# The order of VectorE's modulation sums and routing shift in the first block of a three-block model

## The reference

```python
mod = silu(c) @ w_ada + b_ada                    # 6 x 1024 values
shift1, scale1, gate1, shift2, scale2, gate2 = split(mod, 6)
h = rms_norm(x, norm1_g) * (1 + scale1) + shift1
q, k, v, u, z_gate = split(h @ w_in)
y_attn = attention(q, k, v) @ w_branch_attn
y_pool = pool_mixer(u) @ w_branch_pool
g_attn, g_pool = split(sigmoid(z_gate + b_gate), 2)
mixed = (g_attn * y_attn + g_pool * y_pool) @ w_out
x = x + gate1 * mixed
h2 = rms_norm(x, norm2_g) * (1 + scale2) + shift2
y_moe = experts(h2)                              # router: h2 @ [w_group, w_expert]
x = x + gate2 * y_moe
```

## Time and profile before

| what | value |
|---|---|
| median of 3 timed runs | 1359.34 us (1358.04 to 1361.08) |
| profiled execution | 1357.77 us |
| its span | 1356.0 us |
| busy: TensorE matmul | 1318.7 us (97%) |
| busy: VectorE | 657.4 us (48%) |
| busy: ScalarE | 292.7 us (22%) |
| read from HBM | 359.02 MB, 266 GB/s over the span |
| mean granted TensorE clock | 0.997 |

### The profile page before, as it was taken

One profiled execution on the slowest core, in us unless ns is written; L12 is line 12 of the kernel. 1 busy time (PEld: TensorE's weight loads), 2 busy tenths in 40 slices (PEclk: granted clock), 3 DMA queues, 4 the chain that ended last, 5 costly groups with the idle time before them and its releaser, 6 DMA issues.

```text
span 1356.0 us, 21295 instructions
## 1 busy us (share of the span) xinstructions
PE 1318.7 (97%) x8834; PEld 996.1 (73%) x8834; DVE 657.4 (48%) x1493; ACT 292.7 (22%) x601; POOL 7.8 (1%) x18
## 2 busy tenths in 40 slices
PE   8999899999999999888999999999999999999997
PEld 5999785453443443333688789999998878999997
DVE  6897565121001001000568647775545773867454
ACT  2223102112121121111343611210014361122000
POOL 0000000000000000000000000000000000000000
PEclk9999999999999999999999999999999999999999
DMA  9997797999999999999964054444544414544510
GB/s 389 407 363 260 314 421 308 424 413 422 421 422 421 422 421 422 422 421 421 388 215 141 32 186 156 169 174 159 183 156 141 150 54 155 173 170 161 182 63 32
DMA packets 52099, 364.63 MB, mean 269 GB/s; under 512 B 6161, under 2 KB 6465, under 8 KB 8994
## 3 DMA queue, kind: packets, MB, share of 16 engines
q1 hardware_dynamic: 49392, 355.49, 66.3%
q10 hardware_dynamic: 1890, 5.04, 1.2%
q0 software_dynamic: 720, 2.72, 0.5%
HBM read 359.02 MB, written 2.11 MB: 266 GB/s over the span
## 4 chain that ended last, share of the span: by engine, by line
PE 82%; DMA 13%; DVE 3%; issue 1%; SPq 1%; ACT 0%; DVEq 0%; ACTq 0%
PE bank L1220 31%; PE bank L921 19%; PE bank L667 14%; DMA ring<-in_weights 10%; PE bank L932 3%; PE bank L679 3%; DMA ringx<-in_weights 2%; PE bank L1365 2%; PE bank L1136 2%; PE bank L757 1%; PE bank L906 1%; PE bank L1269 1%; DVE ring L1845 1%; PE bank L1320 1%; PE bank L1346 1%
## 5 line engine op out<-in xcount | busy, mean ns | idle before, releaser
L921 PE MATMUL bank<-ring,cst 128*64 128x512 f32 x600 | 167.6, 595 | 7.1 <-DMA ring<-in_weights 5.7
L1220 PE MATMUL bank<-h,ring 128*128 128x128 f32 x1056 | 134.8, 276 | 1.2 <-DVE small L1818 0.6
L1220 PEld LDWEIGHTS bank<-h,ring 128*128 128x128 f32 x1056 | 126.1, 192 | 2.5 <-issue 2.4
L2165 DVE TENSOR_TENSOR act<-act,bank 128x512 f32<-128x512 f32 (+1 forms) x17 | 11.1, 656 | 239.9 <-PE bank L921 239.9
L667 PE MATMUL bank<-h,ring 128*128 128x256 f32 x576 | 127.1, 380 | 0.1
L667 PEld LDWEIGHTS bank<-h,ring 128*128 128x128 f32 x576 | 108.8, 190 | 15.3 <-issue 0.5
L921 PEld LDWEIGHTS bank<-ring,cst 128*64 128x64 f32 x600 | 52.5, 137 | 91.4 <-issue 89.6
L1220 PE MATMUL bank<-hid,ring 128*128 128x128 f32 x912 | 115.6, 275 | 0.0
L1220 PEld LDWEIGHTS bank<-hid,ring 128*128 128x128 f32 x912 | 108.6, 192 | 0.0
L1220 PE MATMUL bank<-sq,ring 128*128 128x128 f32 x720 | 95.1, 275 | 0.0
L921 PE MATMUL bank<-ringx,cst 128*64 128x512 f32 x256 | 90.3, 595 | 3.8 <-DMA ring<-in_weights 2.3
(11 more groups left out here) (425 smaller groups left out, 1935.7 us busy)
## 6 DMA issues: line engine op xcount, KB each, us to landing
ring<-in_weights SPq DMA_DIRECT2D x251, 1024.0 KB, 10.6
ringx<-in_weights SPq DMA_DIRECT2D x44, 1024.0 KB, 22.9
spare<-in_weights SPq DMA_DIRECT2D x18, 1024.0 KB, 21.2
pool_a<-in_weights SPq DMA_DIRECT2D x9, 1024.0 KB, 23.1
x<-in_weights SPq DMA_DIRECT2D x9, 1024.0 KB, 22.5
ring<-in_weights SPq DMA_DIRECT2D x6, 512.0 KB, 19.6
x<-in_x SPq DMA_DIRECT2D x1, 1024.0 KB, 4.9
pool_a<-in_cst ACTq DMA_DIRECT2D x1, 1024.0 KB, 20.4
```

Of the source, the lines that this page charges most:

```text
L921: ins = e.matmul(g.bank[bank][ex * SLOTS:(ex + 1) * SLOTS, :], stat(m, ex), pair[ex][:, m * 512:(m + 1) * 512], start=first and m == 0, st ...
L1220: ins = e.matmul(u.ap[:, at * P:(at + 1) * P], stat[:, k, :], moving[:, k, :], start=k == 0 and (of == 1 or (b == 0 and first)), stop=k == ...
```

## The change

The change reorders VectorE's instructions. It adds and removes no work, and leaves the other engines' programs and the list of loads alone.

- Gate loop: the modulation sums of tiles 12, 13, 14, 15 stand at j = 1, 3, 4, 5 instead of 1, 3, 5, 7, and at j = 4 behind the bounds.
- The routing shift stands at j = 6 instead of behind the loop, with the sum of tile 16 between its two instructions.
- Attention loop: the sums of tiles 17, 18, 19 ahead of chunks 0, 3, 6, instead of 16 and 17 ahead of chunks 0 and 4.
- Pool loop: the sums of tiles 20 and 21 ahead of chunks 2 and 6, instead of 18 and 19 ahead of chunks 0 and 4.
- Output loop: the sums of tiles 22 and 23 ahead of chunks 0 and 2, instead of 20 to 23 ahead of chunks 0 to 3.

```diff
         if j < 6:
             dve_first_sums(e, g, 6 + j)
-        if j % 2 == 1:
-            dve_ada(e, g, 12 + j // 2)
         if j == 4:
             dve_bounds(e, g)
-
-    modulated(e, g, 15)
-    e.tensor_tensor(g.shift_parts.rearrange("p (k r) -> p k r", k=KC), g.p("w_router").rearrange("p (k r) -> p k r", k=KC),
-                    g.mod[:, 24:32].unsqueeze(2).to_broadcast([P, KC, 36]), ALU.mult).then_inc(s["shift_routed"], 1)
-    e.wait_ge(s["shift_routed"], 1)
-    e.tensor_reduce(g.shift_sum, g.shift_parts.rearrange("p (k r) -> p r k", k=KC), AX.X, ALU.add).then_inc(s["shift_routed"], 1)
+        if j in (1, 3, 4, 5):
+            dve_ada(e, g, (12, 13, 14, 15)[(1, 3, 4, 5).index(j)])
+        if j == 6:
+            modulated(e, g, 15)
+            e.tensor_tensor(g.shift_parts.rearrange("p (k r) -> p k r", k=KC), g.p("w_router").rearrange("p (k r) -> p k r", k=KC),
+                            g.mod[:, 24:32].unsqueeze(2).to_broadcast([P, KC, 36]), ALU.mult).then_inc(s["shift_routed"], 1)
+            dve_ada(e, g, 16)
+            e.wait_ge(s["shift_routed"], 1)
+            e.tensor_reduce(g.shift_sum, g.shift_parts.rearrange("p (k r) -> p r k", k=KC), AX.X, ALU.add).then_inc(s["shift_routed"], 1)
+
     mixed = g.h
     e.wait_ge(s["gated"], 16)
     for oc in range(KC):
-        if oc % 4 == 0:
+        if oc % 3 == 0:
             if oc == 0:
...
-            dve_ada(e, g, 16 + oc // 4)
+            dve_ada(e, g, 17 + oc // 3)
...
     for oc in range(KC):
-        if oc % 4 == 0:
-            dve_ada(e, g, 18 + oc // 4)
+        if oc in (2, 6):
+            dve_ada(e, g, 20 + oc // 4)
...
     for oc in range(KC):
-        if oc < 4:
-            dve_ada(e, g, 20 + oc)
+        if oc in (0, 2):
+            dve_ada(e, g, 22 + oc // 2)
         if oc > 1:
```

## The result

| | kernel before | changed kernel |
|---|---|---|
| median | 1359.33 us (22 runs) | 1361.23 us (22 runs) |
| ratio of the runs | | 1.0014, 95% interval 1.0008 to 1.0020 |
| profiled execution | 1357.77 us | 1361.76 us |
| its span | 1356.0 us | 1360.0 us |
| first load of L584 | 226.05 | 230.07 |

The change makes the kernel slower by 1.9 us, 0.14%, with 1.1 to 2.7 us as the interval. One of the 22 runs of the kernel before took 1515.83 us; without it the median is 1359.32. The lowest runs, 1357.56 and 1359.65, are 2.1 us apart, the two profiled executions 4.0 us. These differences have to be explained, and what lies between them is the instructive part. The last two rows answer: whatever the change does, it does before the experts, and nothing is lost or won behind them.

A forecast was written before the change was run, and what follows sets the result against it. The prediction took the DMA stream to bound the experts, so only TensorE's begin of them counts: 4.6 - 1.5 = +3.1, plus 1.3 for the clock, is +4.4 on 1359.34, so 1363.7 us; range 1358.5 to 1367.6.

The forecast's parts named there:

- One for one through the experts: Experts: the DMA stream never stops, so the kernel's end moves one for one with TensorE's begin of the experts.
- Part 1: Gates and routing shift: TensorE doesn't stop at L798, attention branch and weight stream start earlier, minus 1.45 us.
- Part 2: Attention and pool loops: sums wait for their tiles, tile 21 lands at 179.15, mixture ends at 183.2, 6.6 us later.
- Parts 3 and 4: Output product: chunk 0 held by the last mixture chunks, plus 4.6 us; output loop: stall for scaled chunk 3 gone, minus 1.5.
- the 3 or more given as a sign: Output product: TensorE shows a new wait for L1924, the mixture's last chunks, of 3 us or more.
- The sum of +3.1: Begin of the experts: 4.6 - 1.5 = +3.1 us, 199.67 becoming 202.8, clock not included.
- Part 5: TensorE's clock falls after its idle time before 182.4, in the output run: costs 0 to 1.9 us, taken as 1.3.
- the shift is the same for both: Whole kernel: +4.4 us applies alike to the profiled execution (1357.77) and the timed median (1359.34), giving 1363.7.
- slower by over 0.2%: Whole kernel: slower by more than 0.2%, which is 2.7 us; chance 0.69.
- half of it: Rival: tile 21 lands sooner, without its 1.3 us delay, and the clock doesn't fall: +1.8 us, 1361.1; chance 0.12.
- not slower: Rival: banks hide VectorE's holds, mixture done by 177, experts begin 0.2 us earlier, 1359.1; sign turns at 180; chance 0.12.
- the 2.6 us of start: Weight stream from b2: 2.6 us of start before tiles land every 2.49 us; tile 18 lands 15.07 after b2 leaves.

The follow-up runs named there:

- the filler: Kernel before with two reader-less matmuls (128x512 and 128x256) added on TensorE where it waits for scaled output chunk 3: 1357.83 us, ratio 0.9995.
- the early start: Slot of i15 handed back by the first product of the differences, not the attention branch's first matmul; on the kernel before 1352.70 us, on the changed kernel 1357.04.
- part 1 alone: Changed kernel's gate loop and routing shift, with the three loops over chunks as in the kernel before: 1357.74 us, ratio 0.9990.
- the loops alone: Kernel before with sums 17 to 23 at the new places, gates and routing shift as before: 1363.6 us, ratio 1.0029.
- part 1 with the early start: Kernel before with only the gate and routing shift changes, plus the slot of i15 handed back by the differences: 1350.72 us, ratio 0.9941.

## Why the prediction was right, and where it wasn't

- **One for one through the experts.** Right. In all thirteen profiles, of ten kernels, the time from the first load of L584 to the end is 1129.7 to 1130.4 us, while that load moves between 218.96 and 232.32.
- **Part 1, -1.45.** Right in size. VectorE runs the gates as worked out (sum 14 from 122.68, the shift's reduction from 135.70), L798 doesn't wait, and alone it gives 1.4 us. The begin of the attention branch, 142.17, is as meant too, though the prediction starts it from 143.9 where the earlier trace rows have 143.72.
- **Part 2, the mixture at 183.2.** It ended at 182.44. Sums 18, 19, 20 began within 0.15 us of the forecast. The term that failed is tile 21: I carried its lateness of 1.3 us over from the earlier trace rows. It was not the tile's: in the kernel before b5, the tile ahead of it, landed 3.81 us after tile 20 where others take 2.49, and everything behind was late with it. One packet of instructions lies between the weights there, in the changed kernel none (DMA queues in 174.5 to 177.5, first before, then changed; packets by queue, MB, share):

```profile
q1 hardware_dynamic: 168, 1.25, 100.8%
q8 instruction: 1, 0.02, 2.2%
```

```profile
q1 hardware_dynamic: 180, 1.25, 99.8%
```

  With the packet gone from that place, tile 21 landed at 177.74, before VectorE asked. What sets the end is then VectorE's work behind tile 19, which the prediction's list has, but as a thing beside the tiles. 0.8 us. That tile 22 came as forecast (184.1, landed 184.21) is luck: the packet had only moved, to 179.74, and made that tile late instead.
- **Parts 3 and 4.** The mechanism is the one forecast: output chunk 0 held by the last two mixture chunks, the stream run dry behind tile 22 until the mixture is done, the wait for L1939 gone. The prediction lets the output product begin at once and has no wait of 2.09 us for the bank of pool chunk 3. It cost nothing, as the chunk had to wait for the mixture after its sixth term all the same, but the wait for L1926 was 2.37 us with it, not the 3 or more given as a sign. The sum of +3.1 is +2.1 to +2.3 when measured without a costly fall of the clock (228.13 against 225.84 to 226.05). The 0.9 too much is the 0.8 of tile 21, nearly.
- **Part 5, the clock, +1.3.** The price of a fall, 1.9 us, was read too high, since 20.88 / 3 isn't what 32 matmuls take by themselves: output chunks 6 and 7, 32 of them, took 7.15, and 8.86 is 1.7 more. The fall came in the first profile and cost 1.65 us. In the other it came earlier and cost nothing. The step that failed is the one behind it: "the shift is the same for both", added to a median. The profiled execution of before, 1357.77, is one of its lowest group, and has no costly fall. The median of 1359.3 lies 1.6 us above that group. By the inference from the filler's profile, which no profile of such an execution has confirmed, these are falls behind the wait for tile 23, and the change took away that very wait, so that one risk was put in place of another. What is measured is that the clock gives nothing median against median: +1.9, where the places give +2.1 to +2.3 and the lowest runs are +2.1 apart. Profile against profile it gives +4.0, near the +4.4 forecast, but as a difference between an execution without and one with a costly fall.
- **Range and chances.** 1361.23 lies in the range. The forecast of 1363.7 is 2.5 us too high, and "slower by over 0.2%" had 0.69 where the result, 0.14%, is on the other side of that bound. The rival named "half of it" (+1.8) came nearest, and for its reasons: tile 21 on time, and no fall on top as far as the medians go. Tile 21 and the clock were off the same way, by 0.8 and 1.3 us; the range was wide enough for both.
- **The rival "not slower"** named the point from which it holds, a mixture done by 180. Sums 20 and 21 taken out of the pool loop give 176.94 and a faster kernel, which fits. Its price, -0.2 by the chunk more behind sum 23, wasn't tested, since that kernel moved sums 22 and 23 as well.

## What to carry to other kernels

An instruction that waits for a load holds up everything that is written behind it on its engine, so its place should be read from the landing times of the trace, not from how evenly the work looks spread. Ahead of the last link of a chain even an instruction whose load is there costs its full duration (sum 21: 2.41 us). When a forecast from a profile is put on a median, first see in which group of the timed runs the profile lies, and count a fall of the clock only as the difference between the chances of one before and after. Here the larger gain was neither in VectorE's order nor in its work but in a slot handed back 7 us later than it could be (b2 left at 144.34, and at 137.45 with the early start).

## What the runs showed of the hardware

- A fall of the clock behind a short idle time comes in some executions and not in others. Before the second half of the pool branch TensorE idles 2.1 to 2.3 us in the ten profiles without the early start. The clock fell behind it in six (granted 0.66 to 0.78 in 165 to 170: the three of the kernel before, the first of the changed kernel, part 1 alone, the loops alone) and stayed at 1.00 there in four. It fell also behind 1.90 us (before 199.12, with the filler) and behind 1.10 us (before 197.33, sums 20 and 21 out of the pool loop), where 1.46 to 1.58 us in the three profiles of the kernel before left it up. A fall costs 1.65 to 1.7 us where full matmuls on the path lie behind it (20.40 against 18.75, 8.83 and 8.81 against 7.15), 1.0 us in the short matmuls of the routing (27.33 to 27.39 against 26.36 from output chunk 6 to the experts' loads, in three profiles), and nothing where another wait follows. The larger of these is the size of the steps between the groups of timed runs.
- The first packet of instructions (16 KB) that falls into an unbroken stream of weights makes the stream late, by 1.1 to 1.5 us in nearly all profiles (0.8 in the kernel before with the early start, 0.4 in the second stream of the loops alone), and it stays late until it next pauses. In the profiles of the kernel before one tile lands 3.75 to 3.90 us after the one ahead of it in place of 2.49, after a packet at 173.1 to 175.5; in those of the changed kernel it is tile 22, 3.82 and 3.84, after a packet at 179.4 and 179.7. A second packet before the pause costs nothing: after the one at 196.91 in the kernel before, and after those at 169.34 and 191.07 in part 1 with the early start, no tile takes more than 2.5. In the changed kernel the stream has paused at 182, and the next packet (203.16) costs again, 3.82. What sets when a packet is fetched isn't shown: two profiles of the kernel before have it at 175.47 and 173.08, with TensorE's timelines 0.2 us apart. So the delay moves from tile to tile even without a change.
- A load into an empty queue needs 4.8 to 4.9 us from issue to the last byte (b2 in the kernel before: 144.34 to 149.19), in a full stream each further tile 2.49 us: the 2.6 us of start of the prediction held in the changed kernel too (b2 from 142.79, tile 18 at 157.84: 15.05).
